# A transformer layer on one core: score products of two heads side by side, the second slab rounded where it lands, half of the third tile's finish on ScalarE and GpSimd

## The reference

```python
hin = _rms_norm(x, norm_g[0])
z = hin @ w_in                     # 1024 -> 2964 columns, cut into q, k, v and gates
y_moba, y_ml, y_nsa = ...          # three groups of heads, 4 heads of 64 for moba and nsa
y = concatenate([head_norm(y_moba), head_norm(y_ml) * sigmoid(lo), head_norm(y_nsa)])
x = x + _rms_norm(y @ w_out, norm_g[1])
hm = _rms_norm(x, norm_g[2])
y = square(relu(hm @ w1)) @ w2     # 1024 -> 4096 -> 1024
return x + _rms_norm(y, norm_g[3])
```

## Time and profile before

| | us |
|---|---|
| median of three executions | 606.14 |
| lowest, highest | 605.50, 606.33 |
| the profiled execution, its own time | 605.88 |
| span of the profiled execution | 604.1 |
| TensorE busy in matmuls | 594.5 |
| VectorE, ScalarE, GpSimd busy | 388.0, 300.4, 256.4 |
| mean granted TensorE clock, share of full | 0.997 |

### The profile page before, as it was taken

How to read it: one execution, slowest core, us unless ns; L and a number is a source line. 1 busy time by engine, 2 the same in 40 slices (tenths; PEclk the granted TensorE clock), 3 DMA queues, 4 the chain that set the end, 5 groups by cost and what they waited for, 6 DMA issues and landing times.

```text
span 604.1 us, 8291 instructions
## 1 busy us (share of the span) xinstructions
PE 594.5 (98%) x3099; PEld 485.4 (80%) x3099; DVE 388.0 (64%) x665; ACT 300.4 (50%) x529; POOL 256.4 (42%) x137
## 2 busy tenths in 40 slices
PE   8999999999999999999999999999999999999995
PEld 5898888767867678899878888888888888888884
DVE  6414605265878783883999768586595685771657
ACT  7613423653589933554645536444345255454322
POOL 8553323563095610053357453632723626711611
PEclk9999999999999999999999999999999999999998
DMA  8743281375013820027034250521603404104002
GB/s 331 281 148 131 79 201 73 85 181 187 1 34 79 288 73 0 1 72 278 1 140 139 107 172 1 194 86 43 208 30 139 140 1 147 62 1 174 1 35 106
DMA packets 36580, 67.18 MB, mean 111 GB/s; under 512 B 2876, under 2 KB 23612, under 8 KB 35516
## 3 DMA queue, kind: packets, MB, share of 16 engines
q1 hardware_dynamic: 36236, 66.25, 33.7%
q10 hardware_dynamic: 304, 0.39, 0.3%
HBM read 62.18 MB, written 2.10 MB: 106 GB/s over the span
## 4 chain that ended last, share of the span: by engine, by line
PE 95%; ACT 2%; issue 2%; DVE 1%; POOL 0%; POOLq 0%; ACTq 0%; DVEq 0%
PE ps L1809 20%; PE ps L1811 20%; PE ps L1810 20%; PE ps L2275 7%; PE ps L2277 7%; PE ps L2276 7%; PE ps L2127 2%; PE ps L2142 2%; PE ps L2036 1%; PE ps L2037 1%; ACT probs L946 1%; PE ps L2005 1%; PE ps L1975 1%; PE ps L2203 1%; PE ps L2157 1%
## 5 line engine op out<-in xcount | busy, mean ns | idle before, releaser
L1809 PE MATMUL ps<-xT_h,ring_h 128*128 128x512 f32 (+1 forms) x384 | 144.8, 377 | 0.0
L1811 PE MATMUL ps<-xT_h,ring_l 128*128 128x512 f32 (+1 forms) x384 | 143.3, 373 | 0.0
L1810 PE MATMUL ps<-xT_l,ring_h 128*128 128x512 f32 (+1 forms) x384 | 143.1, 373 | 0.0
L770 POOL TENSOR_TENSOR ring_l<-raw_d,ring_h 128x1024 fp32r<-128x1024 f32 x25 | 67.3, 2700 | 129.9 <-ACT ring_h L1041 129.9
L770 POOL TENSOR_TENSOR ring_l<-raw,ring_h 128x1024 fp32r<-128x1024 f32 x31 | 76.7, 2498 | 77.4 <-DVE xres L1625 38.1
L694 POOL TENSOR_TENSOR ring_l<-raw,ring_h 128x512 fp32r<-128x512 f32 (+2 forms) x26 | 64.2, 2488 | 75.0 <-ACT ring_h L793 75.0
L1719 DVE TENSOR_TENSOR y<-ps,y 128x512 f32<-128x512 f32 x90 | 61.2, 689 | 51.0 <-PE ps L2277 50.6
L1809 PEld LDWEIGHTS ps<-xT_h,ring_h 128*128 128x128 f32 x384 | 72.4, 189 | 15.0 <-issue 2.4
L1811 PEld LDWEIGHTS ps<-xT_h,ring_l 128*128 128x128 f32 x384 | 72.4, 188 | 12.9
L1810 PEld LDWEIGHTS ps<-xT_l,ring_h 128*128 128x128 f32 x384 | 72.4, 189 | 12.3
L2275 PE MATMUL ps<-ring_h,a_h 128*128 128x512 f32 x196 | 76.7, 391 | 0.1
(11 more groups left out here) (277 smaller groups left out, 998.0 us busy)
## 6 DMA issues: line engine op xcount, KB each, us to landing
raw<-in_w_mlp SPq DMA_DIRECT2D x16, 1024.0 KB, 5.5
raw_d<-in_w_mlp SPq DMA_DIRECT2D x16, 1024.0 KB, 6.0
raw<-in_w_groups SPq DMA_DIRECT2D x8, 1024.0 KB, 4.8
xres<-in_x SPq DMA_DIRECT2D x8, 512.0 KB, 6.5
raw<-in_nsa_cmp_w SPq DMA_DIRECT2D x8, 512.0 KB, 6.4
raw<-in_w_groups SPq DMA_DIRECT2D x8, 256.0 KB, 5.0
raw<-in_w_out SPq DMA_DIRECT2D x2, 1024.0 KB, 5.1
raw<-in_w_out SPq DMA_DIRECT2D x4, 512.0 KB, 4.7
```

The costliest lines, as they stand in the source:

```text
L770: nc.gpsimd.tensor_tensor(slot(ring_l, n), slot_source(n), slot(ring_h, n).bitcast(F32), ALU.subtract).then_inc(lo_done, 1)
L1809: nc.tensor.matmul(o, sh, mh, start=start, stop=False)
L1810: nc.tensor.matmul(o, sh, ml, start=False, stop=False)
L1811: return nc.tensor.matmul(o, sl, mh, start=False, stop=stop)
```

## The change

Three edits, which touch different stages.

1. **Attention.** score(s) is cut into products(s) and mask(s). scores(u) issues products(2u), products(2u + 1), mask(2u), mask(2u + 1). In the loop scores(u + 2) stands ahead of everything else of unit u, so that products(2u + 5), with its wait for exponential 2u, comes ahead of the masks, of values or back, and of both transposes of the unit.
2. **The start.** For slab 1 ScalarE rounds x straight from SBUF with the gain as its scale, VectorE computes the low part in one instruction with two SBUF operands, and VectorE, not GpSimd, makes the low part of the weight slab 1.
3. **The finish.** For tile 2 the left half's last step leaves VectorE: ScalarE scales `yg`, GpSimd adds it to `xres` (512 columns each), and the store waits for GpSimd.

```diff
@@ -644,13 +644,16 @@
             sp.dma_start(gain_a[:], norm_g[0, 3:4, :].to_broadcast([P, D])).then_inc(gain3_in, 16)
             for t in range(NT - 1):
                 for k, half in enumerate((1, 0)):
-                    sp.wait_ge(res_ready, 2 * t + k + 1)
+                    if t == NT - 2 and half == 0:
+                        sp.wait_ge(pool_res, 1)
+                    else:
+                        sp.wait_ge(res_ready, 2 * t + k + 1)
                     h0 = 512 * half
                     sp.dma_start(out[0, t * P:(t + 1) * P, h0:h0 + 512], xres[:, t, h0:h0 + 512]).then_inc(stored, 16)
             t = NT - 1
+            sp.wait_ge(res_ready, 2 * t)
+            sp.dma_start(out[0, t * P:(t + 1) * P, own:wide_end], xres[:, t, own:wide_end]).then_inc(stored, 16)
             sp.wait_ge(res_ready, 2 * t + 1)
-            sp.dma_start(out[0, t * P:(t + 1) * P, own:wide_end], xres[:, t, own:wide_end]).then_inc(stored, 16)
-            sp.wait_ge(res_ready, 2 * t + 2)
             sp.dma_start(out[0, t * P:(t + 1) * P, wide_end:D], xres[:, t, wide_end:D]).then_inc(stored, 16)
             sp.wait_ge(stored, 16 * (2 * NT + 1))
 
@@ -695,7 +698,9 @@
                                                    ring_h[r][:, a:a + step].bitcast(F32), ALU.subtract)
                 last.then_inc(lo_done, 1)
 
-            for k in range(NC):
+            for k in (0, *range(2, NC)):
+                if k == 3:
+                    pool.wait_ge(xl_ready, 3)
                 if k % 4 == 3:
                     pool.wait_ge(hi_done, k // 4 + 1)
                 else:
@@ -777,7 +782,10 @@
                     nc.gpsimd.tensor_tensor(yg[:, t, :], y[:, t, 0:512], gain_a[:, 0:512], ALU.mult).then_inc(yg_ready, 1)
                 else:
                     nc.gpsimd.tensor_tensor(yg[:, t, 0:own], y[:, t, 0:own], gain_a[:, 0:own], ALU.mult).then_inc(own_gained, 1)
-            pool.wait_ge(own_scaled, 1)
+                if t == NT - 2:
+                    pool.wait_ge(own_scaled, 1)
+                    nc.gpsimd.tensor_tensor(xres[:, t, 0:512], yg[:, t, :], xres[:, t, 0:512], ALU.add).then_inc(pool_res, 1)
+            pool.wait_ge(own_scaled, 2)
             nc.gpsimd.tensor_tensor(xres[:, NT - 1, 0:own], yg[:, NT - 1, 0:own], xres[:, NT - 1, 0:own], ALU.add).then_inc(pool_res, 1)
 
 
@@ -813,12 +821,20 @@
                 nc.scalar.activation(lv_slab(ring_h, k), lv_slab(raw, k), ACT.Copy).then_inc(hi_done if k % 4 == 3 else hi_first, 1)
 
             def x_high(k):
-                act.wait_ge(x_scaled, k + 1)
-                nc.scalar.activation(xT_h[:, k, :], ps[:, 4 + k % 4, :], ACT.Copy).then_inc(xh_ready, 1)
+                if k == 1:
+                    act.wait_ge(x_land_in[1], 16)
+                    nc.scalar.activation(xT_h[:, 1, :], x_slab(1), ACT.Copy, scale=gain_cols[:, 1:2]).then_inc(xh_ready, 1)
+                else:
+                    act.wait_ge(x_scaled, max(k, 1))
+                    nc.scalar.activation(xT_h[:, k, :], ps[:, 4 + k % 4, :], ACT.Copy).then_inc(xh_ready, 1)
 
             act.wait_ge(x_land_in[0], 16)
             nc.scalar.activation(xf[:], x_slab(0)[:, 0:EARLY_LV * P], ACT.Copy, scale=gain_cols[:, 0:1]).then_inc(xf_ready, 1)
-            for k in range(NC):
+            lv_high(0)
+            x_high(0)
+            x_high(1)
+            lv_high(1)
+            for k in range(2, NC):
                 lv_high(k)
                 x_high(k)
             high_half(2)
@@ -1176,11 +1192,15 @@
                 act.wait_ge(y_sq, 2 * t + 2)
                 act.wait_ge(base_ready, 2 * NT + t + 1)
                 root(SS_Y + 2 * t + 1, ROOT + t, stat[:, BASE + 2 * t:BASE + 2 * t + 1])
+                if t == NT - 2:
+                    act.wait_ge(yg_ready, 2 * t + 2)
+                    act.wait_ge(last_root, 1)
+                    nc.scalar.activation(yg[:, t, :], yg[:, t, :], ACT.Copy, scale=stat[:, R_Y + t:R_Y + t + 1]).then_inc(own_scaled, 1)
             act.wait_ge(own_gained, 1)
-            act.wait_ge(last_root, 1)
+            act.wait_ge(last_root, 2)
             nc.scalar.activation(yg[:, NT - 1, 0:own], yg[:, NT - 1, 0:own], ACT.Copy,
                                  scale=stat[:, R_Y + NT - 1:R_Y + NT]).then_inc(own_scaled, 1)
-            act.wait_ge(pool_res, 1)
+            act.wait_ge(pool_res, 2)
             act.dma_start(out[0, (NT - 1) * P:NT * P, 0:own], xres[:, NT - 1, 0:own]).then_inc(stored, 16)
 
 
@@ -1244,7 +1264,15 @@
                                         ).then_inc(xl_ready, 1)
 
             x_gain(0)
-            for k in range(NC):
+            x_low(0)
+            dve.wait_ge(xh_ready, 2)
+            nc.vector.scalar_tensor_tensor(xT_l[:, 1, :], x_slab(1), gain_cols[:, 1:2], xT_h[:, 1, :].bitcast(F32),
+                                           ALU.mult, ALU.subtract).then_inc(xl_ready, 1)
+            dve.wait_ge(hi_first, 2)
+            nc.vector.tensor_tensor(lv_slab(ring_l, 1), lv_slab(raw, 1), lv_slab(ring_h, 1).bitcast(F32), ALU.subtract
+                                    ).then_inc(xl_ready, 1)
+            x_gain(2)
+            for k in range(2, NC):
                 if k + 1 < NC:
                     x_gain(k + 1)
                 x_low(k)
@@ -1653,9 +1681,14 @@
                 nc.vector.tensor_tensor(gained[:, t % 2, :], y[:, t, 512:1024], gain_a[:, 512:1024], ALU.mult).then_inc(yg_ready, 1)
                 dve.wait_ge(base_ready, 2 * NT + t + 1)
                 c = BASE + 2 * t + 1
-                link(rsqrt1(SS_Y + 2 * t + 1, R_Y + t, ROOT + t, 3 * NT + t + 1, y_sq, 2 * t + 2, stat[:, c:c + 1]))
+                done = rsqrt1(SS_Y + 2 * t + 1, R_Y + t, ROOT + t, 3 * NT + t + 1, y_sq, 2 * t + 2, stat[:, c:c + 1])
+                if t == NT - 2:
+                    done.then_inc(last_root, 1)
+                    dve.wait_ge(last_root, 1)
+                else:
+                    link(done)
                 dve.wait_ge(yg_ready, 2 * t + 2)
-                for half in (1, 0):
+                for half in (1, 0) if t < NT - 2 else (1,):
                     src = gained[:, t % 2, :] if half else yg[:, t, :]
                     xv = xres[:, t, 512 * half:512 * half + 512]
                     nc.vector.scalar_tensor_tensor(xv, src, stat[:, R_Y + t:R_Y + t + 1], xv, ALU.mult, ALU.add
@@ -1795,7 +1828,7 @@
             dve.wait_ge(base_ready, 2 * NT + t + 1)
             c = BASE + 2 * t + 1
             rsqrt1(SS_Y + 2 * t + 1, R_Y + t, ROOT + t, 3 * NT + t + 1, y_sq, 2 * t + 2, stat[:, c:c + 1]).then_inc(last_root, 1)
-            dve.wait_ge(last_root, 1)
+            dve.wait_ge(last_root, 2)
             for k, (n0, n1, held) in enumerate(parts):
                 dve.wait_ge(held_ready, k + 1)
                 nc.vector.scalar_tensor_tensor(xres[:, t, n0:n1], held, stat[:, R_Y + t:R_Y + t + 1], xres[:, t, n0:n1],
@@ -1841,11 +1874,11 @@
                     last = nc.tensor.matmul(ps[:, (J_LV + t) % 8, :], xf[:, t * P:(t + 1) * P], lv_slab(raw, 0), start=True, stop=False)
                 last.then_inc(first_used, 1)
                 for k in range(NC):
-                    pe.wait_ge(xl_ready, k + 1)
+                    pe.wait_ge(xl_ready, k + 2 if k else 1)
                     if k % 4 == 3:
                         pe.wait_ge(lo_done, k // 4 + 1)
-                    else:
-                        pe.wait_ge(lv_low, lv_count(k))
+                    elif k != 1:
+                        pe.wait_ge(lv_low, lv_count(k) - (k > 1))
                     for t in range(0 if k else EARLY_LV, NT):
                         last = mm3(ps[:, (J_LV + t) % 8, :], xT_h[:, k, t * P:(t + 1) * P], xT_l[:, k, t * P:(t + 1) * P],
                                    lv_slab(ring_h, k), lv_slab(ring_l, k), k == 0, k == NC - 1)
@@ -1883,7 +1916,7 @@
                     last.then_inc(job_done, 1)
 
             first_group()
-            pe.wait_ge(xl_ready, 2 * NT)
+            pe.wait_ge(xl_ready, 2 * NT + 1)
             token_group(J_B, C_B, BN)
             pe.wait_ge(consts, 13)
             pe.wait_ge(*reads(J_LV + G_BANK))
@@ -2011,7 +2044,19 @@
                 if u % 2:
                     last.then_inc(ml_o, 1)
 
-            def score(s):
+            def scores(u):
+
+                products(2 * u)
+                products(2 * u + 1)
+                mask(2 * u)
+                mask(2 * u + 1)
+
+            def mask(s):
+                w = (s // 2 % NT + 1) * P
+                nc.tensor.matmul(ps[:, S_BANK[s % 5], w - P:w], identb[:], mask_s[:], start=False,
+                                 stop=True, skip_group_check=True).then_inc(s_done, 1)
+
+            def products(s):
                 u, m = divmod(s, 2)
                 g, i = divmod(u, NT)
                 br, p = PAIRS[g]
@@ -2035,8 +2080,6 @@
                     q, kh, kl = nq_st[:, 2 * p + m], nk_st[:, b], nk_lo[:, b]
                 nc.tensor.matmul(ps[:, bank, 0:n], q[:, i * P:(i + 1) * P], kh[:, 0:n], start=True, stop=False)
```

(14 more changed lines are left out.)

## The result

The changed kernel takes 613.07 us (median of 4 executions, 612.65 to 613.82) against 606.04 before: 7.0 us more. The ratio is 1.0118, with a 95% interval of 1.0101 to 1.0136. The profiled execution took 613.82 us with a span of 612.1, and was thus the slowest of the four; the span is 8.0 longer than before.

The account below looks back on a forecast made before the run. TensorE, with 95% of the chain, was taken to bound the kernel. Attention's 7.2 us lost, less 0.3 for switches, 0.2 at the start and 0.24 at the finish, gave 6.5 more than 605.88: 612.4 us, range 608.6 to 613.9.

Parts of the forecast that it names:

- The waits at u = 13, 17, 21: Attention: products(2u + 5) wait for exponential 2u ahead of values, TensorE idle 1.65, 1.66 and 1.64 us.
- Is the moved work won back?: Attention, u = 13: the 0.56 us of products moved ahead of values stay lost, since ScalarE's work sets the distance between transposes.
- the forecast's 2.2: Attention: values start 2.2 us later at u = 13, 17 and 21, from idle time plus moved products.
- what I let be given back: Attention: part of the 2.2 us delay returns, 0.15 at u = 17 (leaving 2.05); u = 21 is taken as 1.8.
- The intervals that end at units 5 and 9: Attention: u = 5 loses 0.5 us by moved products only; u = 9 loses 0.65, with 0.35 idle.
- the 6 to 7 us that I had named as the sign: Attention stage: 6 to 7 us longer with TensorE's busy time unchanged, as evidence for the forecast.
- The switches: Attention: one transposes-to-products switch fewer per unit, 0 to 0.08 us each; 0.3 taken for the first pair's four units.
- ScalarE catches up: Rival, attention: only idle times count, moved products are won back behind values; 4.6 us more, 610.5; chance 0.18.
- Nothing: Rival: the delays arise but later waits of TensorE take them in; 605.9 us; chance 0.05.
- Faster: Rival, attention: exponential 2u is in time in all units, so no wait and switches count; 603.5 us; chance 0.07.
- The ports: Rival, start or finish: VectorE and GpSimd shut each other out, up to 1.2 us each time; 613.6 us; chance 0.06.
- Start and finish: Start: slab 1's idle weight load shrinks, 0.2 us won (0 to 0.39). Finish: last addition earlier, 0.24 won (0 to 0.27).

Follow-up runs that it names:

- scores together at values only: Kernel before the change, with the scores together in the five units with values and nowhere else: 613.77 us against 605.98, ratio 1.0129.
- apart at values: Changed kernel, but in the five units with values the second score stands between the transposes, as before the change: 607.29 us against 606.12, ratio 1.0019.

## Why the prediction was right

**The sign, the place and the size.** Forecast were 612.4 us, 6.5 over the profiled execution; measured are 613.07, 7.0 over the median before. The range, 608.6 to 613.9, holds it.

**The waits at u = 13, 17, 21.** Forecast were 1.65, 1.66 and 1.64 us idle; the trace has 1.40, 1.39 and 1.40. The forecast took 0.14 from the exponential's end to TensorE, from a copy and its transposes; here it took 190.64 - 190.59 = 0.05. The rest is the way idle time is counted, up to the modelled end of the matmul before: had products(30) been followed by a mask, it would have come 0.24 after their second matmul, as at 190.98 to 191.22, so at 189.09, and from there to 190.64 are 1.55.

**Is the moved work won back?** No, as forecast. Transposes(26) start at 193.74 and the copy that releases transposes(31) ends at 196.91 + 0.51 = 197.42, 3.68 later; before it was 193.68 - 189.85 = 3.83. So the distance is ScalarE's, within 0.15.

**The terms.** From the first product in unit 12, 16 or 20 to values the changed kernel takes 2.18, 2.19 and 2.19 us more: the forecast's 2.2, three times. What was mis-sized is what I let be given back. At u = 17 I had 0.15, and the stretch behind these values, to the first product in unit 20, did not get shorter (6.79 to 6.83). At u = 21 I had 0.4, for no row's sake, and only 0.12 came, in the last interval. Against this, 0.22 was won behind the values of pair 1 (6.97 to 6.75, to the first product in unit 12), which I had not forecast. The intervals that end at units 5 and 9 lost 0.70 and 0.75 against 0.5 and 0.65. In all attention lost 7.74 against 6.9, the 7.2 less 0.3 for switches. That is also above the 6 to 7 us that I had named as the sign. The whole, 7.0 against 6.5, comes closer than this, but single executions differ by as much: the profiled one lay 0.75 above its median.

**The switches.** The 0.08 that a first product lasts longer behind transposes is no real time. Below is a unit with i = 0 from its first product to the next unit's, where nothing waits: first before, then after.

```profile
185.75 0.42 PE L2036 MATMUL ps<-nk_st,nq_st 128*128 128x384 f32 x1
...
186.83 0.47 PE L2036 MATMUL ps<-nk_st,nq_st 128*128 128x512 f32 x1
```

```profile
187.46 0.42 PE L2081 MATMUL ps<-nk_st,nq_st 128*128 128x384 f32 x1
...
188.53 0.48 PE L2081 MATMUL ps<-nk_st,nq_st 128*128 128x512 f32 x1
```

Four products, two masks and two transposes take 1.08 before and 1.07 after, although the products follow each other now. The prediction had 0 to 0.08 for this and took 0.3 for the first four units; it should have been nothing.

**The waits ahead of back** I did not name. Products(2u + 5) of a unit with i = 3 wait for exponential 2u too (0.81, then 0.31 three times), where back had covered it. That the sum came out without it is in part luck: the wait falls where ScalarE's work behind values holds the pair's length anyway, as the run with scores together at values only shows, but I had not looked there. Once values were freed it cost 2.0 us, and a reader who mends only the first place stays 1.2 slower than before.

**The rivals.** "ScalarE catches up" (4.6 us more) is refuted by the intervals of the pairs, and by the 3.2 us that remain once the large waits are gone. "Nothing" and "Faster" fall with the 7.0 us; "Faster" would have needed the exponential in time. "The ports": VectorE's two instructions at the start ran in 0.75 and 0.68, and GpSimd's addition at the finish began at 604.03, behind VectorE's half (603.16 + 0.75 = 603.91); they did not meet, and the price of a meeting stays untested.

**Start and finish.** Forecast were 0.2 and 0.24 won, together 0.44. Measured together: 0.9992 (0.9983 to 1.0000), 0.4 us. By the attention edit alone (7.6) against all three (7.0) it is 0.6, on two occasions. The size agrees; each by itself is below what can be told. The traces give 0.17 at slab 1 in the run with the start alone and about 0.27 at the end in the run with the finish alone.

## What to carry to other kernels

When two engines take turns on short pieces, the price of a wait depends on what stands behind it in the waiting engine's list, and not only on how late the other engine is. A long block such as values here covers a wait that stands behind it in the list, and none that is put ahead of it. Before grouping like instructions, write down for each the semaphore it waits for and what it will now hold back; and take a difference in a matmul's modelled duration for time only if the starts of a whole unit move.

## What the runs showed that I had not expected

- Delays in one chain don't add. Scores together at the five units with values cost 7.8 us, at all 24 units 7.6, although 19 of them cost 1.5 over start and finish (607.29 against 605.76) when the five are left out.
- Orders that look alike differ by 5 us and more: values behind one score and ahead of the other (apart at values, 1.2 over) against values ahead of both (6.2) or behind both (7.0). With values ahead of both, VectorE's row maximum and ScalarE's transposes come late; with values behind both, TensorE's products wait.
- TensorE's first passes took 2.11 to 3.54 us from one execution to the next, so a single profile of this kernel can't tell 1 us at the start. The Trainium skill, TensorE: Matmul & The Clock Gate, section "What's actually happening", says that the moment of the rise varies from run to run. The rows agree, with the spread above.
